# The merge DMAs issued from ScalarE's queue, and another order of the attention steps

## The reference

```python
s = jnp.where(valid, einsum(q, k), -inf); m = max(s); p = exp(s - m); den = sum(p)
o = einsum(p, v) / den;  lse = m + log(den)              # per group
w = jax.nn.softmax(jnp.stack(lses, axis=0), axis=0)      # over the three groups
o = jnp.sum(w[..., None] * jnp.stack(outs, axis=0), axis=0)
```

## Time and profile before

| what | value |
|---|---|
| median of 3 runs | 1864.08 us (1859.25 to 1868.51) |
| the profiled execution's own time | 1868.51 us |
| its span, first to last instruction | 1866.9 us |
| mean granted clock of TensorE | 0.991 |
| PE busy | 1796.4 us, 96% |
| DVE, ACT, POOL busy | 1083.1, 702.7, 486.9 us |

### The profile page before, as it was taken

How to read it: one execution, slowest core, us unless ns; L and a number is a source line. 1 busy time by engine, 2 the same in 40 slices (tenths; PEclk the granted TensorE clock), 3 DMA queues, 4 the chain that set the end, 5 groups by cost and what they waited for, 6 DMA issues and landing times. The chain is left out here.

```text
span 1866.9 us, 27248 instructions
## 1 busy us (share of the span) xinstructions
PE 1796.4 (96%) x9188; PEld 1522.5 (82%) x9188; DVE 1083.1 (58%) x1928; ACT 702.7 (38%) x1598; POOL 486.9 (26%) x578
## 2 busy tenths in 40 slices
PE   6999998999999999999998999989999999999999
PEld 6888887888887888888886888878888888888887
DVE  4362363552734948575766554596555555566786
ACT  5234233243333335352535213453333233334443
POOL 2010001101113515060612000006565556520120
PEclk9999999999999999999999999999999999999999
DMA  7311321422222211111117224322323323278764
GB/s 204 88 44 56 92 75 57 119 67 73 81 72 70 68 33 37 45 45 45 39 51 257 81 80 124 124 73 91 111 85 114 105 95 107 85 260 315 248 217 172
DMA packets 169291, 196.33 MB, mean 105 GB/s; under 512 B 9552, under 2 KB 119472, under 8 KB 168704
## 3 DMA queue, kind: packets, MB, share of 16 engines
q1 hardware_dynamic: 156816, 163.13, 27.3%
q0 software_dynamic: 6128, 21.74, 3.5%
q10 hardware_dynamic: 6272, 10.49, 1.5%
HBM read 150.88 MB, written 44.45 MB: 105 GB/s over the span
## 5 line engine op out<-in xcount | busy, mean ns | idle before, releaser
L2239 PE MATMUL bank<-act_hi,w_hi 128*128 128x512 f32 x568 | 231.8, 408 | 4.0 <-DVE act_lo L1873 3.8
L2241 PE MATMUL bank<-act_hi,w_lo 128*128 128x512 f32 x568 | 224.5, 395 | 0.0
L2240 PE MATMUL bank<-act_lo,w_hi 128*128 128x512 f32 x568 | 224.3, 395 | 0.0
L2239 PE MATMUL bank<-ca,wq 128*128 128x512 f32 x528 | 206.7, 391 | 6.3 <-DVE wq L1984 3.9
L2240 PE MATMUL bank<-ca,wq 128*128 128x512 f32 x528 | 206.2, 390 | 0.0
L2241 PE MATMUL bank<-ca,wq 128*128 128x512 f32 x528 | 206.2, 390 | 0.0
L2239 PE MATMUL bank<-w_hi,act_hi 128*128 128x256 f32 (+1 forms) x576 | 180.6, 314 | 2.5 <-DVE act_lo L1554 2.5
L2241 PE MATMUL bank<-w_hi,act_lo 128*128 128x256 f32 (+1 forms) x576 | 177.2, 308 | 0.0
L2240 PE MATMUL bank<-w_lo,act_hi 128*128 128x256 f32 (+1 forms) x576 | 177.2, 308 | 0.0
L1538 DVE TENSOR_TENSOR w_lo<-w_raw,w_hi 128x1024 fp32r<-128x1024 f32 x38 | 46.1, 1224 | 162.1 <-ACT w_hi L1002 162.1
L2239 PEld LDWEIGHTS bank<-act_hi,w_hi 128*128 128x128 f32 x568 | 108.8, 192 | 28.0 <-DVE act_lo L1873 4.8
(11 more groups left out here) (357 smaller groups left out, 4226.3 us busy)
## 6 DMA issues: line engine op xcount, KB each, us to landing
w_raw<-in_w_in SPq DMA_DIRECT2D x60, 512.0 KB, 4.4
rawd<-in_w_ffn_down SPq DMA_DIRECT2D x99, 256.0 KB, 5.0
rx<-y_scratch SPq DMA_DIRECT2D x77, 256.0 KB, 4.4
wr<-in_w_ffn_gate SPq DMA_DIRECT2D x11, 1024.0 KB, 5.3
wr<-in_w_ffn_up SPq DMA_DIRECT2D x11, 1024.0 KB, 5.4
y_scratch<-sq SPq DMA_DIRECT2D x11, 1024.0 KB, 4.3
y_scratch<-yq SPq DMA_DIRECT2D x33, 256.0 KB, 2.0
gate_scratch<-gbuf ACTq DMA_DIRECT2D x32, 256.0 KB, 2.1
```

The source lines that it names most:

```text
L2239: pe.matmul(ps, lhs_hi, rhs_hi, start=first, stop=False, skip_group_check=onto)
L2240: pe.matmul(ps, lhs_hi, rhs_lo, start=False, stop=False, skip_group_check=onto)
L2241: return pe.matmul(ps, lhs_lo, rhs_hi, start=False, stop=last, skip_group_check=onto)
```

## The change

All statistics and weight DMAs of the merge move from SP to ACT, at fixed steps. `EXP_AT` goes: ACT takes the exponentials of a unit in the step of the unit, right behind that unit's `pt` copy. DVE does `dve_unit` of steps 6 and 7 at the end of the step, behind gains and rotation, and does the first two parts of `merge_mul` in steps 6 and 7 ahead of the gains, the third in step 8 (they were in steps 8, 9 and 12). Three of the weight splits move: tile 5 from step 8 to 7, tile 6 from 10 to 8, tile 7 from 11 to 10, and the next head's tiles from 13 and 14 to 11 and 12. SP's loops are rolled up. The wait of `u_t` for `merge_mul` is now for all three parts. Two `alone(eng)` (one semaphore increment each) go.

```diff
-    HI_A = {6: [4], 8: [5], 10: [6], 11: [7], 13: [8], 14: [9]}
-    EXP_AT = {7: [0], 8: [1, 2]} | {s: UNITS_AT[s] for s in range(9, 16)}
+    HI_A = {6: [4], 7: [5], 8: [6], 10: [7], 11: [8], 12: [9]}
...
# SP
-        for h in range(1, H):
+        with sp.Fori(1, H) as h:
             for k in range(4):
                 load_a(h, k)
             sp.wait_ge(pv_ready, NB * h)
-            alone(sp)
-            store_stats(sp, h - 1)
-            load_stats(sp, h - 1)
             load_vt(h)
             for k in range(4, 8):
                 load_a(h, k)
-            store_weights(sp, h - 1)
-            load_weights(sp, h - 1)
...
# ACT, phase A
                         act.copy(o, i_).then_inc(pt_evac, 1)
-                for j in EXP_AT.get(s, []):
                     if j < NB:
                         act.wait_ge(neg_max, NB * h + j + 1)
...
+                if behind and s == 0:
+                    load_stats(act, h - 1)
                 if behind and s == 1:
                     act_weights(h - 1)
+                if behind and s == 4:
+                    store_weights(act, h - 1)
+                if behind and s == 5:
+                    load_weights(act, h - 1)
...
             act.copy(stat_sb[:, :], pt_ps[0:2 * NU, 0:P]).then_inc(stat_sbd, 1)
+            store_stats(act, h)
...
# ACT, phase B, head 0
+                if not tail and s == 0:
+                    load_stats(act, H - 1)
                 if not tail and s == 1:
                     act_weights(H - 1)
+                if not tail and s == 2:
+                    store_weights(act, H - 1)
+                if not tail and s == 3:
+                    load_weights(act, H - 1)
...
# DVE, inside qk_norm(j)
-                for u in UNITS_AT.get(j, []):
-                    dve_unit(u)
+                if behind and j in (6, 7):
+                    merge_mul(h - 1, j - 6)
...
-                    if behind:
-                        dve.wait_ge(wb_mul, 3 * h - 2 + b // 4)
+                    dve.wait_ge(wb_mul, 3 * h)
...
-            MUL_AT = {8: 0, 9: 1, 12: 2}
...
-                    if behind and s in MUL_AT:
-                        merge_mul(h - 1, MUL_AT[s])
-                    for j in UNITS_AT[s]:
-                        dve_unit(j)
+                    if behind and s == 8:
+                        merge_mul(h - 1, 2)
+                for j in UNITS_AT.get(s, []):
+                    dve_unit(j)
```

More of the change, by code:

```diff
@@ L367, in load_stats @@
         eng.wait_ge(stat_out, 16 * h + 16)
-        alone(eng)
         eng.wait_ge(c_wgt, 3 * h)
@@ L567, in _ @@
                 load_a(h, k)
-            store_weights(sp, h - 1)
-            load_weights(sp, h - 1)
-        def load_b(h, k):
+        with sp.Fori(0, H) as h:
             cols = [C_KB + P * h, C_QB + P * h, C_VB + DV * h + P, C_VB + DV * h,
                     C_RB + DV * h, C_RB + DV * h + P]
[L574 to L585, removed]
             for k in range(TB):
-                load_b(h, k)
+                free(B0 + TB * h + k)
+                load(B0 + TB * h + k, k, w_in[:, :, bass.ds(cols[k], P)])
         def load_m(n):
```

## The result

The kernel after ran at **1883.3 us** (median of five, 1879.3 to 1884.1), the kernel before beside it at 1865.5. The ratio is 1.0095, 95% interval 1.0074 to 1.0117: slower by almost 1%, where 1871.6 and a range up to 1880 were forecast. The two profiled executions stand 12.0 us apart (1868.5 and 1880.5).

What follows compares the result with a forecast made beforehand. PE, 96% busy, was taken to bound the kernel, so only its idle gaps and clock count. -8.0 + 8.7 + 5.1 + 1.7 = +7.5 on 1864.1 gave 1871.6 us, range 1861 to 1880.

Steps and rivals of the forecast that it cites:

- The DMAs on ACT, phase A: Phase A: stores and loads moved to ACT stay hidden, 0 to 0.1 us a head; wb lands 1.4 us early.
- Steps 12 to 14: Phase A, four heads: moved splits add 1.6 us in step 12 and shorten later waits; -2.0 a head, -8.0 us.
- Step 9: Phase A, heads 1 to 3: PE waits 2.9 us for ACT's copy 6 ahead of turn 7; +8.7 us, head 0 none.
- Phase B: Head 0: later wb load delays merge_mul and PE, +5.1 us, a 6.4 us gap; later 2.47 us gap merely shifts.
- The clock: Phase A and phase B's first head: seven half-clock lengths against six in the profiled execution; +1.7 us.
- the rivals: Four alternatives: more half clock (0.25), phase A wb late or another wait (0.14), phase B delay hidden (0.09), faster (0.07).
- rival 2: wb late in phase A too, or another wait in steps 6 to 8: about 1878 us, slower; chance 0.14.

Runs made afterwards that it cites:

- E8: Kernel before's orders with after's transfers on ACT in both phases, ACT's attention loop written out; 1866.1 us, ratio 0.9996 to before.
- E1: Kernel after with ACT's loop over heads 1 to 3 of phase A written out; 1862.4 us, ratio 0.9987 to before.
- E4: Kernel after with phase A's statistics and merge weight DMAs on SP again, phase B's still on ACT; 1867.6 us, ratio 1.0015 to before.
- E5: Kernel after with 231 idle increments ahead of ACT's phase A loop, its body unchanged; 1865.8 us, ratio 0.9992 to before.
- E11: Kernel before with 38 idle increments in steps 2 to 5 of each head in ACT's loop; 1874.3 us, ratio 1.0046.
- E9: Kernel before with 42 idle increments ahead of ACT's attention loop, its body unchanged; 1867.6 us, ratio 1.0009.
- E2: Kernel before with 38 idle increments in ACT's loop just ahead of its wait for the transposed statistics; 1878.4 us, ratio 1.0069.
- E3: Kernel after with SP's v loads held until the statistics are stored, weight loads moving with them, SP's loop written out; 1872.5 us in one execution.
- E7: Kernel before with only the weight splits moved (5, 7, 8 and 9 to steps 7, 10, 11 and 12); 1867.9 us, ratio 1.0005.
- E10: E7 with the third merge product moved from the head of step 12 to the end of step 10; 1852.8 us, ratio 0.9927 to before.
- E6: Kernel before with the order edits alone (splits, exponentials, merge products, units), all DMAs on SP; 1863.0 us, ratio 0.9983.
- E12: E10 with weight split 9 behind the units of step 12 on ACT and DVE; 1844.7 us, ratio 0.9885 to before.

## Why the prediction was wrong

**The step that failed** is "The DMAs on ACT, phase A", which ends at "hidden, 0 to 0.1 a head". It timed the store, the loads and the arithmetic of eleven DMAs one by one and found each covered. All of that was right (E8: nothing). It never asked what their code does to the loop around them. ACT's body grew from 261 to 299 instructions, its back branch lost the code it jumps to, and the fetch stood ahead of the two splits, the work with 0.8 us to spare. The kernels show this from both sides: with the branch taken away (E1), the body shortened (E4) or moved (E5), the gap is gone and the time falls by 16 to 21 us; with 38 idle instructions put into the kernel before (E11), branch cost and packets appear there.

What ACT's branch does, in this case's numbers (first and last instruction of the body, counted from the start of ACT's program in the trace):

| kernel | body | from, to | after the branch, us | q14 packets |
|---|---|---|---|---|
| before | 261 | 277, 537 | 0.23, 0.22 | 32 |
| E9 | 261 | 319, 579 | 0.23, 0.20 | 34 |
| E2, E11 | 299 | 315, 613 | 2.4 to 2.5 | 43 |
| after | 299 | 281, 579 | 5.8, 6.1 | 42 |
| E3 | 299 | 281, 579 | 2.5, 2.7 | 42 |
| E5 | 299 | 512, 810 | 0.21, 0.20 | 33 |

Before against after (starts 277 and 281) says that where the body ends counts, and with it its length; E5 against after (the same length) and E9 against after (the same end) say that its place counts. E9 against E11 does not single out length, though their starts are nearly the same: the four instructions between 315 and 319 may be what decides. The traces show where ACT's code arrives. In before an 8 KB packet of q14 starts 1.0 to 1.6 us after ACT has begun instruction 188, 316 and 444 of this count (138.97 and 140.58, 224.43 and 225.44, 281.42 and 282.55 us), and from there to the end of the loop none comes; in E5 the same holds at 188, 316, 444, 572 and 700, within 0.6 to 1.9 us. These places are 128 instructions apart.

The Trainium skill (Runtime: NRT & Kernel Launch, section "Instruction fetch mechanics") has the rule that I had not drawn on: an engine holds two pages of 256 instructions, and a taken branch to a target outside them must wait for a DMA of that page. The traces agree that it is a fetch and that both length and place matter. If pages began where this count begins, the rule would fail: after's body (281 to 579) would lie in the same two pages as before's (277 to 537). But the count begins at the first instruction in the trace, which need not begin a page. With a page beginning at 316 to 319, and others 256 before and behind, every row of the table comes out: the bodies of before, E9 and E5 begin in the page of their branch or the one ahead of it, those of after, E3, E2 and E11 one page further back. This placing was fitted to the rows afterwards; the packets at 316 and 572 agree with it, and no run was made to test it. As an estimate from the rule of the Trainium skill, with this place, a body of 299 instructions stalls at 42 of 256 possible starts and one of 261 at 4; after's would have escaped had it begun five to eight instructions earlier.

**The second half of its price** is what the last sentence of that step dismissed: "What SP no longer waits for (its loads of v and of weights come earlier) frees nothing". It frees the v loads, and the weight loads behind them, into the very moment of the fetch. E3 cuts 5.8 and 6.1 us to 2.5 and 2.7 and takes 10.8 us off after's median (one execution). Where there is no fetch they harm nothing (E5).

**The other steps.**
- *Steps 12 to 14*: right. -2.0 a head forecast; 4.5 us of waits became 2.4. Step 14's 1.1 measured 1.07 (0.94 in head 0), step 12's 1.6 measured 1.32 (1.11 in head 0).
- *Step 9*: right in mechanism, place and heads, and none in head 0; 2.9 us forecast, 2.15 measured, 6.5 in place of 8.7. Step 10's 0.9 us was missed. It is absent in E7 and E10, which have the splits but not the early products, the later units and the moved exponentials, so it belongs to these; which of the three was not separated.
- *Phase B*: right in its cause. The first gap is 4.93 us where 6.4 were forecast: counted from the head's end, `wb` landed 1.1 us earlier than worked out. The later gap did not merely shift: 2.47 us became 0.21, because TensorE itself, 2.2 us slower at half clock behind the first gap, came that much later to the products that wait for the masks. So half clock cost little there, and the forecast counted both it and the gap that it filled. The stretch grew by 1.9 us in after's trace, 3.2 from E6 to E4 (4.6 in medians), against 5.1.
- *The clock*: seven half-clock lengths forecast in these stages. After's trace has seven, but by luck: four came with the two gaps of the failed step, one with step 9, none with steps 12 to 14, two with phase B. Without the branch three were seen (E1) or one (E5). At 1.7 us each that is the largest error beside the failed step.

So without the failed step, E1 and E5 stand at -0.13% and -0.08% (-2.4 and -1.5 us), where +7.5 us was forecast. That is 9 to 10 us between. The profiled executions show the terms: E1's stands 5.5 us under before's where 7.5 over was forecast, 13.0 between. The clock was counted four lengths (6.8 us) too dear, phase B's two gaps 3.9, step 9 2.6 and steps 12 to 14 1.4, and step 10's 1.5 us were missed: 13.2 in all. The two errors, this one and the failed step, had opposite signs, and the overlooked one, 17 to 21 us, was twice the other. None of the rivals was the case; rival 2 allowed for another wait, but in steps 6 to 8 and for 6 us in all.

## What to carry to other kernels

Before work is moved onto an engine that runs a hardware loop, count the instructions of the loop's body and what the move adds, DMA issues with their address arithmetic above all (eleven DMAs added 38 instructions here), mind that the body's place counts as much as its length, and look at what stands right behind the back branch: a fetch there cost 2.5 us, and 6 beside heavy transfers, each time round. The signs are an idle time "issue" at the first instruction of a body, and a packet count on the instruction queue that grows with the number of turns. Writing the loop out was the simplest remedy, and E12 shows the better use of a spare microsecond: long work that nobody waits for belongs behind the short copies that TensorE waits for.

## What the runs showed of the hardware that was not expected

- A taken branch of ACT was followed within 0.23 us or, with its target gone, 2.4 to 6.1 us, depending on length, place and on other transfers at that moment. VectorE's loop of 294 instructions showed no such cost in either kernel.
- Instructions that do nothing and are never waited for (78 ns each on ACT) made a kernel 0.5% slower in E11 and another 1.0% faster than it was in E5, by where they put the rest.
- Half clock followed waits: E12 without a gap over 1.1 us in phase A has none there, and E12's mean granted clock is 0.996 against before's 0.991. Not every wait drew one: E5's three of 2.17 us in step 9 drew none. And half clock costs little where it fills a wait that would have come anyway (phase B: 2.2 us of it, and the wait of 2.47 us became 0.21).
